# Subtracted softmax attention: the first product moved to GpSimd, a third place for the probabilities, and eight head norms done in two batches

## The reference

```python
def diff_attention(q, k, v, lam):      # 8 heads, two softmaxes each, block of 128 queries
    def block(qi):
        s = jnp.einsum("bhcqd,bhckd->bhcqk", qi, kf) * (dh ** -0.5)
        a = jax.nn.softmax(s, axis=-1)
        return jnp.einsum("bhqk,bhkd->bhqd", a[:, :, 0] - lam * a[:, :, 1], vf)
...
    o = diff_attention(q, k, v, lam)
    o = rms_norm(o, subln, LN_EPS) * (1.0 - lambda_init)
    return o.reshape(B, S, C_MIX).astype(x.dtype) @ w_out
```

## Time and profile before

| | |
|---|---|
| median of 3 runs | 2616.57 us (2614.85 to 2617.04) |
| the profiled execution | 2613.11 us, of which its span is 2611.3 us |
| busy: PE, DVE, ACT, POOL | 95%, 46%, 26%, 72% of the span |
| mean granted PE clock | 0.976 |

### The profile page before, as it was taken

The page is one execution under the profiler, slowest core; times in us unless marked ns, Lnnn a source line. Parts: engine busy times, 40 slices in busy tenths (PEclk is TensorE's granted clock), DMA queues, the critical chain, the costliest instruction groups (busy, mean ns, idle before and its releaser), DMA issues.

```text
span 2611.3 us, 32318 instructions
## 1 busy us (share of the span) xinstructions
PE 2477.3 (95%) x11154; PEld 1898.5 (73%) x11154; DVE 1204.8 (46%) x1598; ACT 689.4 (26%) x1242; POOL 1867.8 (72%) x1505
## 2 busy tenths in 40 slices
PE   7988989999999978889999999999999999999998
PEld 6745768888767843568888767866888878668886
DVE  7486463330161788563330177444523465453323
ACT  2265233330021146133330033134110131450101
POOL 8703468888867930568888878753999897449996
PEclk9989999999999999899999999899999999999999
DMA  4201112222212210112222213211222222112222
GB/s 169 89 1 41 41 65 98 97 96 98 94 65 97 89 41 1 49 65 96 96 96 97 97 65 106 85 57 49 89 97 96 89 98 81 56 49 97 97 96 89
DMA packets 57543, 207.07 MB, mean 79 GB/s; under 512 B 6512, under 2 KB 6896, under 8 KB 57200
## 3 DMA queue, kind: packets, MB, share of 16 engines
q1 hardware_dynamic: 55872, 199.87, 22.0%
q10 hardware_dynamic: 1584, 5.96, 0.6%
HBM read 203.71 MB, written 2.10 MB: 79 GB/s over the span
## 4 chain that ended last, share of the span: by engine, by line
PE 77%; DVE 13%; POOL 4%; issue 3%; ACT 2%; DMA 0%; POOLq 0%; DVEq 0%; ACTq 0%
PE bank L687 21%; PE bank L688 21%; PE bank L689 21%; PE bank L717 3%; PE bank L762 3%; POOL w_hi L2255 2%; PE bank L790 2%; PE bank L811 2%; DVE negmax L1767 2%; POOL w_lo L2258 2%; DVE region L1714 2%; PE bank L876 1%; DVE moving_lo L1931 1%; DVE branch_lo L1694 1%; DVE x L1940 1%
## 5 line engine op out<-in xcount | busy, mean ns | idle before, releaser
L2255 POOL TENSOR_TENSOR w_hi<-ring,unit 128x512 fp32r<-128x512 f32 x750 | 846.4, 1128 | 664.6 <-PE bank L689 526.6
L2258 POOL TENSOR_TENSOR w_lo<-ring,w_hi 128x512 fp32r<-128x512 f32 x750 | 1033.2, 1378 | 58.7
L687 PE MATMUL bank<-moving_hi,w_hi 128*128 128x512 f32 x1962 | 778.9, 397 | 33.5 <-DVE moving_lo L1931 20.3
L688 PE MATMUL bank<-moving_lo,w_hi 128*128 128x512 f32 x1962 | 771.9, 393 | 0.0
L689 PE MATMUL bank<-moving_hi,w_lo 128*128 128x512 f32 x1962 | 770.9, 393 | 0.0
L687 PEld LDWEIGHTS bank<-moving_hi,w_hi 128*128 128x128 f32 x1962 | 372.6, 190 | 128.2 <-issue 26.4
L689 PEld LDWEIGHTS bank<-moving_hi,w_lo 128*128 128x128 f32 x1962 | 373.0, 190 | 79.3
L688 PEld LDWEIGHTS bank<-moving_lo,w_hi 128*128 128x128 f32 x1962 | 373.1, 190 | 77.7 <-issue 1.5
L2202 DVE TENSOR_TENSOR region<-region,bank 128x512 f32<-128x512 f32 x64 | 39.7, 682 | 278.5 <-PE bank L689 278.5
L1913 DVE SCALAR_TENSOR_TENSOR region<-x,bank 128x512 f32<-128x512 f32 x32 | 21.3, 686 | 285.9 <-PE bank L689 285.7
L1767 DVE TENSOR_REDUCE negmax<-bank 128x2 f32<-128x1024 f32 (+2 forms) x96 | 98.1, 1022 | 118.3 <-PE bank L766 88.3
(11 more groups left out here) (258 smaller groups left out, 3399.3 us busy)
## 6 DMA issues: line engine op xcount, KB each, us to landing
ring<-in_weights SPq DMA_DIRECT2D x375, 512.0 KB, 3.2
x<-in_x_t ACTq DMA_DIRECT2D x4, 512.0 KB, 8.5
out<-region SPq DMA_DIRECT2D x8, 256.0 KB, 2.1
region<-in_tables ACTq DMA_DIRECT2D x1, 1312.0 KB, 6.0
region<-in_tables ACTq DMA_DIRECT2D x1, 1024.0 KB, 5.9
region<-in_p_t ACTq DMA_DIRECT2D x2, 512.0 KB, 4.9
region<-in_tables SPq DMA_DIRECT2D x1, 320.0 KB, 10.4
small_w<-in_small_w ACTq DMA_DIRECT2D x1, 320.0 KB, 5.9
```

The source lines that it names most:

```text
L687: pe.matmul(bank, lhs[0], rhs[0], start=start, stop=False, skip_group_check=True)
L688: pe.matmul(bank, lhs[0], rhs[1], start=False, stop=False, skip_group_check=True)
L2255: pool.tensor_tensor(w_parts[0][:, s, at], ring[:, s, at], unit[:, 0:1].broadcast_to([P, BLK // 2]), ALU.mult).then_inc(split_hi, 1)
L2258: pool.tensor_tensor(w_parts[1][:, s, at], ring[:, s, at], w_parts[0][:, s, at].bitcast(F32), ALU.subtract).then_inc(split_ready, 1)
```

## The change

It does four things, all in the C heads.

- `prob` and `rope_tmp` become one tile `work` of six, and a turn's pair of probabilities goes to place t%3 of three (`blend_slot`).
- The blend is cut in three: `invert` on DVE (reciprocals, and one product with the pair 1 and minus lambda), the first tile times its factor on GpSimd (`scale_first`), and `blend` on DVE. DVE's order becomes maximum n, blend n-2, invert n-1. ACT copies the transposes of turn n-2 after its exponentials of turn n, where it copied those of n-1.
- The output of a head and its square are both read from the bank by ACT (`finish`), in place of the copy on DVE and the later square.
- The norms go in two groups of four heads: the sums are products with 32 columns of ones into 32 rows each of one bank, one square root and one `inverse` for each group, and a product with a repeated column of the identity spreads each head's row over 128 partitions of a bank, from where DVE applies it.

The programs of PE for scores, transposes and values, and `AHEAD`, keep their order.

```diff
-        prob = sb("prob", [P, 4, S])
-        rope_tmp = sb("rope_tmp", [P, 2, S])
+        work = sb("work", [P, 6, S])
+        prob, rope_tmp = work[:, 0:4, :], work[:, 4:6, :]
...
+        def blend_slot(t, c):
+            return work[:, 2 * (t % 3) + c, :]
...
@@ PE, heads_blended and heads_c
-                        mm = pe.transpose(psum[4 + t % 2][:, kt * P:kt * P + P], prob[:, 2 * (t % 2), kt * P:kt * P + P], ident)
+                        mm = pe.transpose(psum[4 + t % 2][:, kt * P:kt * P + P], blend_slot(t, 0)[:, kt * P:kt * P + P], ident)
...
                 for n in range(C_HEADS):
-                    if n >= 2:
-                        pe.wait_ge(std_ready, T["std"][("C", n - 2)])
-                    sum_squares(None, psum[4 + n % 2], 1, lambda _: square[:, n, :], lambda _: ("C", n))
+                    g, rows = n // 4, slice(32 * (n % 4), 32 * (n % 4) + 32)
+                    pe.wait_ge(squared, T["squared"][("C", n)])
+                    mm = pe.matmul(psum[g][rows, :], ones[:, 0:32], square[:, n, :], start=True, stop=True)
+                    if n % 4 == 3:
+                        mm.then_inc(summed, 1)
+                for n in range(C_HEADS):
+                    g, row = n // 4, 32 * (n % 4)
+                    pe.wait_ge(c_inverse, g + 1)
+                    if n >= 4:
+                        pe.wait_ge(normed, T["normed"][("C", n - 4)])
+                    pe.matmul(psum[4 + n % 4][:], ident[:, row:row + 1].broadcast_to([P, P]), rstd[:, g, :], start=True,
+                              stop=True).then_inc(c_spread, 1)
...
@@ ACT, attention_c
+                def finish(u):
+                    g = GROUP_AT[u]
+                    act.wait_ge(weighed, g + 1)
+                    act.activation(mix[:, u[1], :], psum[6 + g % 2], ACT.Copy).then_inc(attended, 1)
+                    act.activation(square[:, u[1], :], psum[6 + g % 2], ACT.Square).then_inc(squared, 1)
+
+                for n, (u, i) in enumerate(turns):
+                    t = TURN_AT[(u, i)]
+                    act.wait_ge(turned, max(t - 2, first_c))
+                    for c in range(2):
+                        act.wait_ge(maxed, 2 * t + c + 1)
+                        at = 2 * (t % 4) + c
+                        act.activation(blend_slot(t, c), psum[2 * (t % 2) + c], ACT.Exp, bias=negmax[:, at:at + 1],
+                                       accum_out=rowsum[:, at:at + 1]).then_inc(exped, 1)
+                    if n >= 2:
+                        copy_turned(*turns[n - 2])
+                    if i == 2 and n > 2 * ST:
+                        finish(units[n // ST - 2])
...
@@ DVE, heads_c
-                attention([u for u in UNITS if u[0] == "C"], lambda u: mix[:, u[1], :], blend=True)
+                def invert(n):
...
+                    dve.wait_ge(exped, 2 * t + 2)
+                    link(dve.reciprocal(rownorm[:, at:at + 2], rowsum[:, at:at + 2]))
+                    dve.tensor_tensor(rownorm[:, at:at + 2], rownorm[:, at:at + 2], neg_lam[:, 4:6], ALU.mult).then_inc(inverted, 1)
+
+                def blend(n):
...
+                    dve.wait_ge(p0_scaled, n + 1)
+                    dve.scalar_tensor_tensor(out=blend_slot(t, 0), in0=blend_slot(t, 1), scalar=rownorm[:, at + 1:at + 2],
+                                             in1=blend_slot(t, 0), op0=ALU.mult, op1=ALU.add).then_inc(scaled, 2)
+
+                for n, turn in enumerate(turns):
+                    t = TURN_AT[turn]
+                    dve.wait_ge(scored, t + 1)
+                    dve.tensor_reduce(negmax[:, 2 * (t % 4):2 * (t % 4) + 2], banks[:, 2 * (t % 2):2 * (t % 2) + 2, :], AX_X, ALU.max,
+                                      negate=True).then_inc(maxed, 2)
+                    if n >= 2:
+                        blend(n - 2)
+                    if n >= 1:
+                        invert(n - 1)
...
@@ POOL
+            def scale_first(units):
+                turns = [(u, i) for u in units for i in range(ST)]
+                for n, turn in enumerate(turns):
...
+                    pool.wait_ge(inverted, n + 1)
+                    pool.tensor_tensor(blend_slot(t, 0), blend_slot(t, 0), rownorm[:, at:at + 1].broadcast_to([P, S]),
+                                       ALU.mult).then_inc(p0_scaled, 1)
```

More of the change, by code:

```diff
@@ L601, in build @@
         for n in range(C_HEADS):
-            for t in ("squared", "summed", "std", "normed"):
-                T[t].add(("C", n))
+            T["squared"].add(("C", n)), T["normed"].add(("C", n))
+        for g in range(2):
+            T["summed"].add(("C", g)), T["std"].add(("C", g))
         plan_ln(2), plan_ln(3)
@@ L1530, in heads_c @@
             def heads_c():
[L1531 to L1542, removed]
+                attention_c([u for u in UNITS if u[0] == "C"])
+                for g in range(2):
+                    deviation(("C", g), psum[g], P, col("eps_ln"), g)
+                split_mix(1, ("qkC", 15), range(C_HEADS))
             def gain(i, n):
@@ L1719, in normalize, with attention @@
                     behind(n)
-            def attention(units, evacuate, blend=False, causal=False, masked=False, gate=None, first=()):
+            def attention(units, evacuate, causal=False, masked=False, gate=None, first=()):
                 turns = [(u, i) for u in units for i in range(ST)]
[L1724 to L1734, removed]
                 def normalised(u, i):
@@ L1769, in attention @@
                     if n:
-                        (blended if blend else normalised)(*turns[n - 1])
-                    before = units[max(n // ST - 1 - blend, 0)]
-                    if i == 3 - 2 * blend and n > ST * (1 + blend) and before[0] != "slc":
+                        normalised(*turns[n - 1])
+                    before = units[max(n // ST - 1, 0)]
+                    if i == 3 and n > ST and before[0] != "slc":
                         finish(before)
@@ L1776, in attention @@
                         pending.pop(0)[1]()
-                (blended if blend else normalised)(*turns[-1])
-                for u in units[-1 - blend:]:
-                    finish(u)
+                normalised(*turns[-1])
+                finish(units[-1])
                 for _, step in pending:
@@ new lines, in heads_c @@
+                last = len(turns) - 1
+                blend(last - 1)
+                invert(last)
+                blend(last)
+                for g in range(2):
+                    dve.wait_ge(std_ready, T["std"][("C", g)])
+                    link(dve.transpose(rstd[:, g, :], std[:, g, :]))
+                    link(dve.reciprocal(inverse_tmp[:, :], rstd[:, g, :].rearrange("p (b r) -> p b r", r=32)[:, :, 0]))
+                    ins = dve.transpose(rstd[:, g, :], inverse_tmp[:, :].unsqueeze(2).broadcast_to([P, S // 32, 32]))
+                    ins.then_inc(c_inverse, 1)
+                    dve.wait_ge(c_inverse, g + 1)
```

56 lines of the change are left out of this document (43 added, 13 removed).

## The result

The changed kernel takes 2701.61 us (median of 4 runs, 2695.43 to 2712.16) against 2615.91 us for the kernel before: a ratio of 1.0332, 95% interval 1.0298 to 1.0365. It is slower. The profiled execution has a span of 2693.6 us, 82.3 more than that of before. Nearly all of it lies in the C heads: from the first maximum to the first use of the projection it was 1075.85 - 945.0 = 130.9 us, and now it is 1158.04 - 945.8 = 212.2, 81.4 more.

A forecast was written before the change was run, and what follows sets the result against it. The prediction took DVE to bound the C heads before, PE close behind, and a closed ring after. Turns and tail +47, clock +33, norms -5 made +75 on 2613.11, 2688; the median 3.5 above gave 2692 us, range up to 2730.

The forecast's parts named there:

- The ring: C heads: blend, transposes, values, scores, maximum and next blend run in series, 4.64 us a turn at PE's upper clock level.
- GpSimd costs nothing: C heads: GpSimd's product, taken as 1.2 us, has 3.6 us of room, so moving it costs and brings nothing.
- The clock: C-head turns and tail: PE's pauses lower its granted clock 56% of the time, slow turns 7.09 us, +33 us.
- the upper level's sum: C heads, first to last maximum with PE's clock at 1.00: 134.8 us against 89.8, +45.0.
- The tail: Last maximum to the end of the values: 11.8 us at the upper clock level against 9.7, +2.1.
- The norms: End of values to projection's first use, 31.3 us before: -8 at the upper clock level, +12 at the lower, -5 taken.
- the sign: Sign that the forecast is right: 24 to 30 us from the last values to the projection's first use.
- The sum: Whole kernel: +47 + 33 - 5 = +75 us on the profiled 2613.11, giving 2688, and 2692 for the median.
- The clock that holds: Rival, chance 0.16: pauses of 2 us in the C heads do not lower PE's clock; +39, 2656 us.
- every turn is at the lower level: Rival, chance 0.12: PE's clock never rises inside the C-head stage, 7.09 us a turn; +132, 2749 us.
- The ring that is no ring: Rival, chance 0.05: scores of turn n+3 overtake the waiting transposes of turn n, 2.6 us a turn; 2600 us.
- DVE's busy share in the turns: Sign in the C-head stage: DVE's busy share falls from over 90% to about half.

The follow-up runs named there:

- experiment 1: Changed kernel with PE issuing scores three turns ahead, not two: 2590.77 us, ratio 0.9913 to the kernel before.
- 6: Changed kernel with the blend put back to one turn behind, GpSimd's product still in its way: 2622.2 us, ratio 1.0025 to the kernel before.
- experiment 3: Changed kernel with two more fp32 products of 512 columns per turn filling PE's pause: 2657.01 us, ratio 1.0158 to the kernel before.
- 2: Changed kernel with the blend's first product moved from GpSimd back to DVE: 2699.1 us, ratio 1.0317 to the kernel before.
- 4: Kernel before with only the change to the norms (sums, roots, inverses, spreads): 2604.35 us, ratio 0.9959.
- 5: Changed kernel with scores three turns ahead and the blend's first product back on DVE: 2594.76 us, ratio 0.9925 to the kernel before.
- 7: Kernel before with scores three turns ahead and nothing else: 2643.53 us, ratio 1.0112.
- 8: Kernel before with scores three turns ahead and a third place of probabilities: 2643.51 us, ratio 1.0111.
- 9: Changed kernel with scores three turns ahead but two places of probabilities, not three: 2615.2 us, ratio 1.0005 to the kernel before.
- 10: Changed kernel with scores three turns ahead and the first four heads' norm moved ahead of the last values: 2591.97 us, ratio 0.9919 to the kernel before.
- experiment 11: Kernel before with scores three turns ahead, three places of probabilities and ACT's copy of the transposes two turns behind: 2615.8 us, ratio 1.0006.

## Why the prediction was right

It said 2692 us, in a range of 2650 to 2730, and it was 2701.61. The direction and the mechanism of the ring stood as written; that the total came within 10 us is in part luck, since two wrong sizes went against each other. The runs took each part:

- *The ring.* The steps are 4.64 us at the upper level, the sum worked out from the earlier trace rows. It was shown and not only argued: opened at PE's end (experiment 1) it gave 111 us back, opened at DVE's end (6) 79. With the clock held (3) the turns take 137.5 us against a sum of 134.8. In each opened kernel the clock comes back as well, so 111 and 79 are the ring and the clock together.
- *GpSimd costs nothing.* Right: its product took 1.04 us (I took 1.2) and ended at 1003.12, while its blend starts at 1007.87; with the product on DVE the time was the same (2).
- *The clock.* The mechanism was right (experiment 3) and the size too small. I took 56% of the time at the lower level, borrowed from the norms of before, where PE's pauses have other lengths (1.30 and 1.92 us in the earlier trace rows); it was 72%. With 72% the prediction's own sum gives +46, of which 3 are for the tail. A slow turn is 6.89 us, not 7.09: the transposes add 0.42 by the starts (0.91 for 0.49) and not 0.55, the values 0.89 and not 0.95. Of the +33, 2.4 were for the tail, so 31 for the turns; measured, the extra over the upper level's sum is 180.2 - 134.8 = 45.4 us, or 42.7 over the 137.5 of experiment 3. That is the term that was off most.
- *The tail* was 12.2 us from the last maximum to the end of the values, at a mean clock of 0.70, against 11.8 at the upper level and 14.2 with its share of the clock.
- *The norms.* -11.5 us (19.8 for 31.3), not -5, and outside the 24 to 30 that I gave as the sign. The eight sums were mis-sized: 2.29 us for all, where I counted 7.6. They ran side by side: their 16 records last 0.59 us each, 9.5 together, and lie within 2.29 us, with the clock at 1.00. The Trainium skill (TensorEngine Tiling, When to Use Tiling) gives four-fold column tiling for 32 output columns, which the prediction named and kept out of its sum; the trace agrees with it, at 2.29 us against 8 x 0.95. The rest of the difference is the clock: I expected part of the norms at the lower level, and their mean was 0.91.
- *The sum*: +45.0 and +45.4 for the turns, +2.5 for the tail, -11.5 for the norms: +81.4, where the prediction had +45, +33, +2 and -5, +75. The clock's term came out 12 us too small and the norms 7 us too dear, and these went against each other.
- *The rivals.* The clock that holds was wrong for this kernel, and experiment 3 is that rival made real: 2657 us, where 2656 was worked out. That every turn is at the lower level was wrong too: the clock rose again and again, as in the step from 1006.73 to 1011.37. The loop that the Trainium skill tells of (TensorE: Matmul & The Clock Gate, HAM oscillation) has waits that are longer than the work between them. In the ring here the pause of 2.06 us is shorter than PE's work of 4.64 - 2.06 = 2.58 us or more, so the prediction read that page too widely, and no run here shows such a loop. The ring that is no ring needed scores that overtake; when the program itself puts them ahead, the time is 2591, where 2600 was worked out, because the turns went to 2.48 us on average (2.51 each from 965 us on), a little under the 2.57 that I read as PE's work.
- DVE's busy share in the turns fell to 64.22 of 181 us, 35%; I had said about half, which holds at the upper level alone (64.04 of 137 us in experiment 3, 47%).

What the change needed shows in the stage's two parts: from the first to the last maximum (the turns), and from there to the first use of the projection (the tail and the norms), each from the profiled execution.

| kernel | turns, us | rest, us | median, us |
|---|---|---|---|
| before | 89.8 | 41.1 | 2615.91 |
| the change | 180.2 | 32.0 | 2701.61 |
| 1: three ahead | 77.0 | 32.5 | 2590.77 |
| 2: product on DVE | 188.4 | 32.0 | 2699.1 |
| 3: pause filled | 137.5 | 32.4 | 2657.01 |
| 4: before, norms alone | 90.0 | 29.3 | 2604.35 |
| 5: three ahead, product on DVE | 80.3 | 29.7 | 2594.76 |
| 6: blend one behind | 105.1 | 30.2 | 2622.2 |
| 7: before, three ahead | 117.3 | 41.5 | 2643.53 |
| 8: 7 with three places | 117.4 | 41.5 | 2643.51 |
| 9: 1 with two places | 99.2 | 31.7 | 2615.2 |
| 10: 1, first norms early | 78.6 | 30.2 | 2591.97 |
| 11: 8, copy two behind | 89.1 | 41.0 | 2615.8 |

Every kernel with the new norms gains about 9 to 12 us in its rest, whatever its turns do. So of the 24 us that experiment 1 gains on the kernel before, about 13 are from the turns and 9 from the rest, and experiments 6 and 9, which stand near the kernel before in time, lose 15 and 9 us in the turns. The look-ahead loses without the copy moved (7, 8) and without the third place (9). With both, but with the old blend, it gains nothing (11): DVE is the bound there, as before. The product's move to GpSimd is not what that kernel lacks most: with the product still on DVE, but the blend cut and two behind and the outputs copied by ACT (5), the turns are 8.8 us shorter than in experiment 11, and the product's move brings 3.3 more (1). How the 8.8 us divide between the blend and the copies, no run tells.

## What to carry to other kernels

When a step is moved one turn later on one engine, follow its result through the fixed order of the next engine back to the moved step, and count how many turns the loop spans: the time of a turn is the loop's sum divided by that number, or the busiest engine's work, whichever is longer. (All the rings here span one turn; the division for a longer one is argued, not shown.) Distances on the engines go together: here a blend one turn later wanted the scores one turn further ahead, and those wanted the copies and the places one turn further apart; each of these left behind closed a ring of its own (the change, 7 and 8, 9). Before blaming a slow engine, look whether anyone waited for it; and where PE pauses in each turn, price the turn at both clock levels, because the pause can cost about as much again as it lasts (2.25 us more in a slow turn, for a pause of 2.06). And split a total by stage before calling two kernels equal: a loss in one part and a gain in another can cancel (9).

## What the runs showed that I had not expected

- Extra PE work made the kernel faster: 64 products in the pauses took 45 us off (2701.61 to 2657.01), since the mean clock of the turns went from 0.64 to 0.98.
- At steps of 6.89 us with a pause of 2.06 the clock mostly stayed at the lower level, and the mean clock differed from run to run (0.953 to 0.946), with spans that differed by 17 us.
- Eight fp32 sums with 32 output columns and 512 moving columns took 2.29 us in all, and the same number with 128 output columns 8.83 (the spreads, at a mean clock of 0.81 and in step with DVE).
